# Gated linear attention: state on TensorE, wide score products, and dummy bf16 products in the steps with preparation

## What is computed

```python
def step(state, inp):
    qi, ki, vi, gi = inp
    cum = jnp.cumsum(gi, axis=2)
    diff = cum[:, :, :, None, :] - cum[:, :, None, :, :]
    decay = jnp.where(causal, jnp.exp(jnp.where(causal, diff, 0.0)), 0.0)
    scores = jnp.einsum('bhid,bhijd,bhjd->bhij', qi, decay, ki)
    last = cum[:, :, -1:, :]
    out = (jnp.einsum('bhij,bhjv->bhiv', scores, vi)
           + jnp.einsum('bhid,bhdv->bhiv', qi * jnp.exp(cum), state))
    state = (jnp.exp(last[:, :, 0, :, None]) * state
             + jnp.einsum('bhjd,bhjv->bhdv', ki * jnp.exp(last - cum), vi))
    return state, out
```

## Time and profile before

| | |
|---|---|
| median of 3 runs | 3348.65 us (3347.36 to 3349.76) |
| profiled execution | 3347.46 us |
| its span | 3345.8 us |
| mean granted TensorE clock | 0.920 of 2.4 GHz |
| busy: TensorE, its weight loads, VectorE, ScalarE, GpSimd | 90%, 72%, 49%, 29%, 21% |
| instructions | 39719 |

### The profile page before, as it was taken

The page is one execution under the profiler, slowest core; times in us unless marked ns, Lnnn a source line. Parts: engine busy times, 40 slices in busy tenths (PEclk is TensorE's granted clock), DMA queues, the critical chain, the costliest instruction groups (busy, mean ns, idle before and its releaser), DMA issues. The chain is left out here.

```text
span 3345.8 us, 39719 instructions
## 1 busy us (share of the span) xinstructions
PE 3018.4 (90%) x15196; PEld 2401.4 (72%) x15196; DVE 1653.0 (49%) x2819; ACT 982.9 (29%) x1921; POOL 688.4 (21%) x442
## 2 busy tenths in 40 slices
PE   6999788788999999978999799988899997999888
PEld 4767788336888888866758688866777676887766
DVE  4170773213413413332488763476524787634865
ACT  3241220111000000020267442075102674421751
POOL 1233000002333333313112301402141113014021
PEclk8999555798999999989999899999999998999989
DMA  3111000201111021113112101203231120012032
GB/s 106 35 32 35 1 1 23 82 6 63 38 57 51 32 64 51 32 69 105 27 38 70 32 1 42 79 8 126 89 106 27 39 75 26 1 51 70 7 126 89
DMA packets 78801, 168.41 MB, mean 50 GB/s; under 512 B 14848, under 2 KB 33808, under 8 KB 78096
## 3 DMA queue, kind: packets, MB, share of 16 engines
q1 hardware_dynamic: 70160, 140.61, 12.6%
q10 hardware_dynamic: 8448, 25.18, 2.7%
HBM read 128.00 MB, written 20.97 MB: 45 GB/s over the span
## 5 line engine op out<-in xcount | busy, mean ns | idle before, releaser
L296 PE MATMUL psum<-H,ffn_W 128*128 128x512 f32 x672 | 262.8, 391 | 12.8 <-POOL ffn_W L1328 11.1
L297 PE MATMUL psum<-H,ffn_W 128*128 128x512 f32 x672 | 262.4, 390 | 0.0
L298 PE MATMUL psum<-H,ffn_W 128*128 128x512 f32 x672 | 262.3, 390 | 0.0
L1326 POOL CAST ffn_W<-ffn_W 128x1024 fp32r<-128x1024 f32 (+1 forms) x84 | 69.3, 825 | 891.7 <-PE psum L298 447.5
L1623 DVE TENSOR_SCALAR_CACHE_REDUCE MB<-OM,tk_mid 128x512 bf16<-128x512 f32 (+2 forms) x192 | 184.3, 1010 | 2.3
L1592 ACT ACTIVATE MB<-OM,tk_mid 128x384 bf16<-128x384 f32 (+2 forms) x192 | 157.0, 818 | 51.8 <-DVE tk_mid L1620 48.5
L1402 DVE TENSOR_SCALAR ffn_Y<-ffn_G,ffn_par 128x1024 f32<-128x1024 f32 x21 | 22.1, 1052 | 297.6 <-ACT ffn_G L1391 297.6
L482 POOL TENSOR_TENSOR tk_W<-tk_W 128x1024 fp32r<-128x1024 f32 (+1 forms) x38 | 78.5, 2068 | 425.9 <-ACT tk_W L434 425.9
L1328 POOL TENSOR_TENSOR ffn_W<-ffn_W 128x1024 fp32r<-128x1024 f32 (+1 forms) x84 | 161.8, 1926 | 6.7
L296 PEld LDWEIGHTS psum<-H,ffn_W 128*128 128x128 f32 x672 | 126.8, 189 | 40.1 <-POOL ffn_W L1328 11.5
L298 PEld LDWEIGHTS psum<-H,ffn_W 128*128 128x128 f32 x672 | 126.7, 189 | 26.7
(11 more groups left out here) (416 smaller groups left out, 7647.4 us busy)
## 6 DMA issues: line engine op xcount, KB each, us to landing
OM<-in_w_feat SPq DMA_DIRECT2D x34, 512.0 KB, 4.4
tk_W<-in_w_feat SPq DMA_DIRECT2D x22, 512.0 KB, 3.7
ffn_W<-in_ffn_w_gate SPq DMA_DIRECT2D x21, 512.0 KB, 3.5
ffn_W<-in_ffn_w_val SPq DMA_DIRECT2D x21, 512.0 KB, 3.5
ffn_W<-in_ffn_w_down SPq DMA_DIRECT2D x42, 256.0 KB, 2.6
OM<-MB ACTq DMA_DIRECT2D x64, 128.0 KB, 2.6
OM<-OM ACTq DMA_DIRECT2D x64, 128.0 KB, 3.0
fin_W<-in_w_out SPq DMA_DIRECT2D x4, 2048.0 KB, 10.5
```

The costliest lines, as they stand in the source:

```text
L296: pe.matmul(out, a1, b1, start=start, stop=False)
L297: pe.matmul(out, a1, b2, start=False, stop=False)
L298: return pe.matmul(out, a2, b1, start=False, stop=stop)
L1326: pool.tensor_copy(w1, w).then_inc(rounded, 1)
```

## The change

Within `gla_stage` alone:

- The score products take all 128 rows and both heads at once: `QW` gets a second head's place, each head's rows hold its weighed queries and the other rows are zero. One product of 128 columns per level stands where two of 64 stood, and one of two columns for the diagonal. TensorE waits for `mixed` and a new count `spread` first.
- `weigh` on VectorE weighs the queries in place (count `lifted`); ScalarE copies each head's rows from there to `QW` (`part_heads`, two copies for each level). For pass 3 it does so again from the half tiles of pass 2 (`spread_at`: c = 4 to 6 of pass 2, c = 0 to 2 of pass 3).
- GpSimd clears the rows of `QW` that a pass leaves stale (12 memsets, count `cleared`).
- The state: ScalarE writes the diagonal matrix of the decays (`fade`), TensorE multiplies it with the state into bank 7 and adds the update there, and ScalarE copies the result to `ST` (`carry`). VectorE's state update and its resets are gone; chunk 0 of a pass has neither `fade` nor the state's part of the output.
- The exponentials of level 64 and of KL take their reference as ScalarE's bias (`bend_first`, `bend_state`: 8 pieces of 64 columns and 4 of 128), and VectorE no longer subtracts those two references.
- ScalarE's order in a step is now: `fade`, `carry`, at c = 3 and 7 the turned keys, the wait for the output and its copy, the preparation, the spreading for pass 3.
- In the 15 steps with preparation TensorE multiplies a constant read as bf16, eight times 128 x 512, into a bank that nobody reads, between the scores and the wait for `placed`.
- The start-up `spin` waits for six weights, not seven.

```diff
@@ gpsimd
+                for v in CLEARED:
+                    p, half = v // 2, v % 2
+                    if p:
+                        pool.wait_ge(out_done, NT * (p - 1) + CH * (half + 1))
...
+                    for h, r in enumerate(stale[p]):
...
+                        pool.memset(QW[r, :, at, h, :], 0.0).then_inc(cleared, 1)
@@ vector: weigh
-                    own(dve.tensor_tensor(QW[:, n, CH * (u % 2):CH * (u % 2 + 1), :]
-                                          .rearrange("p c (m w) -> p c m w", w=b),
-                                          w4[:, :, :, b:2 * b], q4[:, :, :, b:2 * b], ALU.mult))
...
+                    dve.tensor_tensor(w3[:, :, up], w3[:, :, up], q3[:, :, up], ALU.mult).then_inc(lifted, 1)
+                    own(dve.tensor_tensor(w3[:, :, down], w3[:, :, down], k3[:, :, down], ALU.mult))
@@ vector: the loop
                         place(step)
-                        if c < NT - 1:
...
-                            dve.wait_ge(upd_done, step + 1)
-                            for h, r in enumerate(rows):
...
-                                last = dve.scalar_tensor_tensor(
-                                    ST[r, (c + 1) % 2, v], ST[r, c % 2, v], EL[r, c:c + 1],
-                                    kit.psum[r, 7, v], ALU.mult, ALU.add)
-                            last.then_inc(upd_taken, 1)
@@ scalar
+                def bend_first(u):
...
+                    for m in range(CH):
+                        c = CH * (u % 2) + m
+                        act.activation(w3[:, m, 64:P], c3[:, m, 64:P], ACT.Exp, bias=NR[:, c:c + 1])
+                        last = act.activation(w3[:, m, 0:64], c3[:, m, 0:64], ACT.Exp, scale=-1.0, bias=c3[:, m, 63:64])
+                    last.then_inc(weights, 1)
...
+                def bend_state(u):
...
+                    for m in range(CH):
+                        last = act.activation(k3[:, m, :], c3[:, m, :], ACT.Exp, scale=-1.0, bias=c3[:, m, P - 1:P])
+                    last.then_inc(weights, 1)
...
+                def part_heads(v, n):
...
+                    act.wait_ge(lifted, NL * min(v, 4 + half) + n + 1)
+                    act.wait_ge(cleared, 2 * len([x for x in CLEARED if x <= v]))
...
+                    for h, r in enumerate(rows_in[p]):
+                        last = act.activation(QW[r, n, CH * half:CH * (half + 1), h, :]
+                                              .rearrange("p c (m w) -> p c m w", w=b), w4[r, :, :, b:2 * b], ACT.Copy)
+                    last.then_inc(spread, 1)
...
+                def fade(p, c):
...
+                    act.activation(FADE[:, n % 2, :], ident, ACT.Copy, scale=EL[:, c:c + 1]).then_inc(fading, 1)
+
+                def carry(p, c):
+                    act.wait_ge(upd_done, (NT - 1) * p + c + 1)
...
+                    for h, r in enumerate(rows_in[p]):
+                        v = slice(h * 64, (h + 1) * 64)
+                        last = act.activation(ST[r, (c + 1) % 2, v], kit.psum[r, 7, v], ACT.Copy)
+                    last.then_inc(upd_taken, 1)
...
                         step = NT * p + c
+                        if c < NT - 1:
+                            if c:
+                                fade(p, c)
+                            carry(p, c)
+                        if c % CH == CH - 1 and prep_at(p, c - 1):
+                            keys_turned(prep_at(p, c - 1)[0])
                         act.wait_ge(out_done, step + 1)
...
@@ tensor
+                    pe.wait_ge(mixed, min(2 * p + c // CH, 5) + 1)
+                    pe.wait_ge(spread, NL * (2 * p + c // CH + 1))
                     for n in range(NL):
-                        for h, r in enumerate(rows_in[p]):
-                            pe.matmul(kit.psum[:, 2 * (step % 2) + h, n * 64:(n + 1) * 64], KW[r, n, at],
-                                      QW[r, n, c, :], start=True, stop=True)
...
+                        pe.matmul(bank[:, n * P:(n + 1) * P], KW[:, n, at],
+                                  QW[:, n, c, :, :].rearrange("p h m -> p (h m)"), start=True, stop=True)
...
+                            if c:
+                                n = (NT - 2) * p + c - 1
+                                pe.wait_ge(fading, n + 1)
+                                pe.matmul(kit.psum[:, 7, 0:P], FADE[:, n % 2, :], ST[:, c % 2, :], start=True, stop=False)
+                            pe.matmul(kit.psum[:, 7, 0:P], KLT[:, c * P:(c + 1) * P], V[:, c, v_at:v_at + P],
+                                      start=c == 0, stop=True).then_inc(upd_done, 1)
...
+                        if prep_at(p, c):
+
+                            constants_bf = kit.spin.bitcast(BF16)
+                            for _ in range(8):
+                                pe.matmul(kit.psum[:, 4 + c // CH, :], constants_bf[:, 0:P],
+                                          constants_bf[:, HALF:2 * HALF], start=True, stop=True)
                         pe.wait_ge(placed, step + 1)
```

More of the change, by code:

```diff
@@ L896, in levels_of, with spread_at, weight_count @@
         return ((0, 1), (2, 3), (4, 5, 6))[part]
+    def spread_at(p, c):
+        if p == 2 and CH <= c < CH + 3:
+            return 6, c - CH
+        if p == 3 and c < 3:
+            return 7, c
+        return None
+    def weight_count(r):
+        n = r % N_R + 1
+        return N_Z * (r // N_R) + (n if n < TAIL else n + 1) + 1
+    CLEARED = (0, 1, 4, 5, 6, 7)
     with ExitStack() as mem:
@@ L906, in gla_stage @@
         EL = sbuf(nc, mem, "gla_EL", [P, NT])
+        NR = sbuf(nc, mem, "gla_NR", [P, NT])
         KLT = sbuf(nc, mem, "gla_KLT", [P, S])
@@ L988, in place @@
                         dve.wait_ge(out_done, step - 1)
-                    bank = kit.pair(step % 2).rearrange("p (h n) -> p h n", h=2)
+                    bank = kit.pair(step % 2)
                     first = own.n
@@ L1012, in _ @@
                 for p in range(NP):
[L1013 to L1018, removed]
-                    for c in range(NT):
-                        step = NT * p + c
-                        place(step)
-                        if c < NT - 1:
[L1023 to L1026, removed]
-                            dve.wait_ge(upd_done, step + 1)
-                            for h, r in enumerate(rows):
-                                v = slice(h * 64, (h + 1) * 64)
-                                last = dve.scalar_tensor_tensor(
-                                    ST[r, (c + 1) % 2, v], ST[r, c % 2, v], EL[r, c:c + 1],
-                                    kit.psum[r, 7, v], ALU.mult, ALU.add)
-                            last.then_inc(upd_taken, 1)
-                            dve.wait_ge(upd_taken, (NT - 1) * p + c + 1)
+                    for c in range(NT):
+                        place(NT * p + c)
+                        if p >= 2 and c == 0:
+                            dve.wait_ge(out_done, NT * p)
+                            dve.memset(ST, 0.0).then_inc(state_set, 1)
                         if prep_at(p, c):
@@ L1075, in _ @@
                             prep(*prep_at(p, c))
-                            u, part = prep_at(p, c)
-                            if part == 2:
-                                keys_turned(u)
+                        if spread_at(p, c):
+                            v, part = spread_at(p, c)
+                            for n in levels_of(part):
+                                part_heads(v, n)
             @block.tensor
@@ L1086, in scores @@
                     at = slice(c * P, (c + 1) * P)
+                    bank = kit.pair(step % 2)
+                    pe.wait_ge(mixed, min(2 * p + c // CH, 5) + 1)
+                    pe.wait_ge(spread, NL * (2 * p + c // CH + 1))
                     for n in range(NL):
-                        for h, r in enumerate(rows_in[p]):
-                            pe.matmul(kit.psum[:, 2 * (step % 2) + h, n * 64:(n + 1) * 64], KW[r, n, at],
-                                      QW[r, n, c, :], start=True, stop=True)
-                    for h, r in enumerate(rows_in[p]):
-                        last = pe.matmul(kit.psum[:, 2 * (step % 2) + h, NL * 64:NL * 64 + 1], QK[r, at],
-                                         heads[r, 2 * p + h:2 * p + h + 1], start=True, stop=True)
+                        pe.matmul(bank[:, n * P:(n + 1) * P], KW[:, n, at],
+                                  QW[:, n, c, :, :].rearrange("p h m -> p (h m)"), start=True, stop=True)
+                    last = pe.matmul(bank[:, NL * P:NL * P + 2], QK[:, at], heads[:, 2 * p:2 * p + 2],
+                                     start=True, stop=True)
                     last.then_inc(scored, 1)
```

141 lines of the change are left out of this document (81 added, 60 removed).

## The result

The changed kernel takes 3409.1 us (median of four, 3406.6 to 3412.4) against 3349.2 for the kernel before: 1.0177 times as long, with a 95% interval of 1.0159 to 1.0195. It is slower, by 60 us, where the forecast had 30. The side was right and so was the wait that decides; the size was not, and the time lies above the range.

What follows compares the result with a forecast made beforehand. The gated attention stage, at half clock, was taken as the only part affected. Preparations of 174.7 and other steps of 78.8 make 253.5 instead of 222.3 us; 3347.46 + 31.2 gives forecast 3379, range 3335 to 3405.

Steps and rivals of the forecast that it cites:

- What bounds the kernel, and that only this stage changes: Gated attention stage: half clock, TensorE's own 6.57 us limiting steps without preparation; everything outside the stage untouched.
- the start-up: Before the stage's first output: zero change, between -1.5 and +2.5 us.
- `fade` behind the preparation holds TensorE: Preparing steps: TensorE's update waits for `fade`, queued behind ScalarE's preparation; idle of 5.06, 4.98 and 3.76 us.
- The dummies uncovered: Preparing steps: no wait covers the dummy products, so 14 of 15 sets lie on TensorE's path, 1.84 us each.
- Rival B: Dummies hidden because VectorE's masks come later: 26 us less, 3353, no change; chance 0.08.
- The bursts: TensorE's work in a step: 3.65 us at full rate, 5.49 with dummies, plus 2.1 for a clock fall.
- The clock falls in every preparing step and returns after each: Idle of 3.8 to 5.1 us drops TensorE's clock 15 times, 2.1 us lost each, 31.5 us in all.
- Rival A: The clock survives the idle in preparing steps: 31.5 us less, 3348, no change; chance 0.10.
- Rival D: The clock never returns to full rate, so each of 31 steps takes its burst twice: 3485 us; chance 0.04.
- rival C: Faster: ScalarE's pieces on fewer partitions or columns much cheaper, idle stays at 2 us, no falls: 3309; chance 0.18.
- four with two levels of head copies 5.55: Four steps where ScalarE only copies queries for pass 3: 5.55 us each, 22.2 together, no clock fall counted.
- five preparations: The 15 preparing steps of the stage: 3 x 35.3 + 2 x 34.4 = 174.7 us.

## Why the prediction was right in kind and short in size

- **What bounds the kernel, and that only this stage changes:** right. All but 6.7 us of one execution's difference is there, and the start-up cost 0.9, called zero.
- **`fade` behind the preparation holds TensorE:** right, the step that decides. Idle of 5.75, 5.49 and 4.69 where 5.06, 4.98 and 3.76 were worked out; 88.4 us by one releaser; and it goes when `fade` moves (77 us). The terms that read rows held: eight pieces 1.92 for 1.92, four exponentials 1.22 for 1.24, `fade` 0.40 for 0.39. From the Trainium skill's 93 ns for a pointer and 0.833 ns a column (ScalarE: Activation LUTs, What ACT_TABLE_LOAD costs) 0.24 is the estimate for the 64-column piece, and the trace agrees (355.38 to 355.62). The head copies did not hold: 0.43 for 0.31, which is 0.5 of the 0.69 missing in part 0; the rest is the way in and out of ScalarE, 0.34 and 0.15 where 0.22 and 0.05 were taken.
- **The dummies uncovered:** right. 14 x 1.84 was the term, the run without them gained 25.9 in the stage. Rival B is out: the masks were done at 360.56 and TensorE asked at 366.17.
- **The bursts:** right in the sum, by two errors that cancel. The ten bursts after parts 0 and 1 take 7.5 on average (step less idle), 5.49 + 2.1 = 7.6 was forecast. At full rate one is 5.17, a little less than 5.49, and a fall is 2.4, a little more than 2.1.
- **The clock falls in every preparing step and returns after each:** right, 15 of 15. Rival A is out. Its hope that eight dummies would carry the clock over the gap is refuted by 21 falls with them and 20 without. Rival D is out because the rate returns, and rival C because the 64-column pieces cost 0.24, the value taken, and the head copies more than a whole piece, not less.
- **The step that failed: "four with two levels of head copies 5.55" and what stands with it.** The sum put falls only where ScalarE prepares. The spreading steps were given full rate without being asked for their idle. By the prediction's own prices it was 1.9 (0.66 + 1.24), short of its shortest row that fell, 2.79; it measured 2.60 (the four copies 0.48 more, the ways in and out 0.22), and that does drop the clock, in these steps one after another. A step of 7.8 loses 0.7 in idle and 1.5 in rate, and the step behind can start at half rate too (4.8 for 3.3, 7.0 for 4.3). Together the last twelve are 21.2 over. Filling their idle gave 13.5 us of it back in the stage, with the copies still slow, and that is the clock's part. The other mis-sized term is the head copy, 0.43 where 0.31 was taken: their new order alone, with the falls still there, gave 9.5 us of the stage back.
- **The rest:** five preparations 180.5 for 174.7. Idle is 8.5 more, made up in part by the shorter bursts and by the step into chunk 7.
- **The range** ended 4 us short of the measured time. Its sides were made from falls at 1.4 to 2.9 and pieces at their bounds, and held no case for more falls than 15, nor for head copies over 0.31. Four to six more falls at 2.4, or a copy price with a side at the whole duration of one (0.41) instead of at the distance of another form, would have held it. Its own sides, added up, reach 3399.5 and not 3397 (12 + 3 + 3 + 2.5 above 3379), which changes nothing here.

What is still open is which idle survives. The runs show falls at 2.60, 2.70, 2.37 and, with 0.46 just ahead of it, at 2.17; and that of two steps with the same 0.95 and 0.88 one falls; with dummies in the long waits four falls come after idle of 1.33 at the most. So the length of the last idle alone does not decide, and nothing here was made to settle what does.

## What to carry to other kernels

When work moves to another engine's queue, look first at what stands ahead of it there: one instruction moved from behind a preparation to ahead of it made this kernel 77 us faster. Dummy products paid here only right in front of a wait about as long as they are, or longer; where nothing was waited for they were on the path at full price. And if a sum gives each idle of one kind a loss of clock, go through all steps for their idle, the small ones too, with the price of each engine's instruction at its upper bound.

## What the runs showed of the hardware

- With idle of 2.60 ahead of an update the granted clock went from 2.4 to 1.2 GHz (1.00 until 571.5 and 0.50 from 571.9 on, in the changed kernel), and so it did with 2.37 (372.08, `fade` first without dummies). The Trainium skill (TensorE: Matmul & The Clock Gate, Why this matters for your kernels) allows gaps of up to about 3 us; the measurements here are stricter, and decide. Falls also came after idles of 0.31 and 0.89 (464.14, `fade` first, dummies in front of waits). A fall cost 2.4 us in this stage.
- Without any idle of note, fp32 products of 32 rows by 64 columns lost the full rate within two steps, and 81.5 us of them in 84 didn't regain it; products of 128 rows by 128 columns regained it after every fall within the stage, mostly within one set of scores, but after the idles of 2.17 (579.85) and 3.52 (610.00) of the changed kernel only behind the second. Whether rows or columns decide wasn't tried.
- ScalarE's copies of 256 columns start 0.43 apart when they alternate between two ranges of partitions, and 0.31 to 0.33 apart within one range; ordering 98 copies by range took 6.0 us off ScalarE's busy time (40.8 to 34.8).
